# Six norms ahead of the linears: squares summed into columns of tokens, root and reciprocal taken on those, the result spread by a matmul

## The reference, cut to what matters

```python
def rms_norm(x, g=None):
    xf = x.astype(F32)
    y = xf * lax.rsqrt(jnp.mean(xf * xf, axis=-1, keepdims=True) + EPS)
    ...
def modulate(h, shift, scale):
    return h * (1.0 + scale) + shift
...
h @ w_in
```

## Time and profile before

| what | value |
|---|---|
| median of 3 runs | 3646.12 us (3642.33 to 3648.9) |
| the profiled execution | 3642.8 us, its span 3641.0 us |
| mean granted TensorE clock | 0.909 of full speed |
| TensorE matmul busy | 3077.7 us (85%), 15844 instructions |
| weight loads busy | 2512.0 us (69%) |
| VectorE busy | 1320.7 us (36%) |
| ScalarE busy | 1020.9 us (28%) |
| GpSimd busy | 961.4 us (26%) |

### The profile page before, as it was taken

One profiled execution on the slowest core, in us unless ns is written; L12 is line 12 of the kernel. 1 busy time (PEld: TensorE's weight loads), 2 busy tenths in 40 slices (PEclk: granted clock), 3 DMA queues, 4 the chain that ended last, 5 costly groups with the idle time before them and its releaser, 6 DMA issues. The chain is left out here.

```text
span 3641.0 us, 40685 instructions
## 1 busy us (share of the span) xinstructions
PE 3077.7 (85%) x15844; PEld 2512.0 (69%) x15844; DVE 1320.7 (36%) x1888; ACT 1020.9 (28%) x1443; POOL 961.4 (26%) x308
## 2 busy tenths in 40 slices
PE   2888976588998998899989999998967777988697
PEld 1667876476887887779547767876856665778475
DVE  7264636523155126040133164113544445101412
ACT  2244234213311211322023232223322223323432
POOL 0101211022222322643013334432423222330132
PEclk7889986688999999999999999999989888999798
DMA  4101410011133135422102243222200001220021
GB/s 176 40 1 58 157 58 1 1 49 56 54 137 127 58 108 198 145 81 84 43 22 82 81 179 136 101 82 74 89 22 0 0 0 47 93 88 24 22 84 58
DMA packets 48509, 265.33 MB, mean 73 GB/s; under 512 B 5380, under 2 KB 6660, under 8 KB 28420
## 3 DMA queue, kind: packets, MB, share of 16 engines
q1 hardware_dynamic: 48384, 263.63, 20.3%
HBM read 261.51 MB, written 2.10 MB: 72 GB/s over the span
## 5 line engine op out<-in xcount | busy, mean ns | idle before, releaser
L378 POOL TENSOR_TENSOR shared_w_lo<-stage,shared_w_hi 128x2048 fp32r<-128x2048 f32 (+2 forms) x179 | 783.6, 4378 | 1968.1 <-ACT shared_w_hi L351 1955.9
L351 ACT CAST shared_w_hi<-stage 128x2048 fp32r<-128x2048 f32 (+2 forms) x179 | 319.6, 1787 | 519.7 <-PEq L332 147.9
L418 PE MATMUL f0i_acc<-norm_b_hi,shared_w_hi 128*128 128x512 f32 x704 | 186.1, 346 | 27.8 <-PEq L332 14.5
L418 PE MATMUL f0i_acc<-norm_b_lo,shared_w_hi 128*128 128x512 f32 x704 | 184.8, 344 | 0.0
L418 PE MATMUL f1i_acc<-norm_e_hi,shared_w_hi 128*128 128x512 f32 x352 | 140.1, 398 | 9.5 <-DVE norm_e_lo L526 8.0
L418 PEld LDWEIGHTS f0i_acc<-norm_b_hi,shared_w_hi 128*128 128x128 f32 x704 | 110.2, 193 | 46.9 <-issue 25.0
L418 PE MATMUL f1i_acc<-norm_e_lo,shared_w_hi 128*128 128x512 f32 x352 | 138.9, 394 | 0.0
L618 DVE TENSOR_TENSOR ffn_hidden<-f0i_acc,ffn_gate 128x512 f32<-128x512 f32 (+1 forms) x44 | 22.5, 553 | 307.5 <-PE f0i_acc L418 307.5
L418 PE MATMUL f0i_acc<-norm_b_hi,shared_w_lo 128*128 128x512 f32 x704 | 130.3, 338 | 0.0
L608 ACT CAST ffn_hi<-ffn_hidden 128x768 f32 (+3 forms) x44 | 32.0, 728 | 330.2 <-DVE ffn_hidden L618 330.2
L418 PEld LDWEIGHTS f0i_acc<-norm_b_lo,shared_w_hi 128*128 128x128 f32 x704 | 110.6, 193 | 16.1
(11 more groups left out here) (536 smaller groups left out, 7262.4 us busy)
## 6 DMA issues: line engine op xcount, KB each, us to landing
stage<-in_w_f0i SPq DMA_DIRECT2D x22, 1024.0 KB, 4.8
stage<-in_w_f1i SPq DMA_DIRECT2D x22, 1024.0 KB, 4.8
mod_slots_d<-in_w_mod SPq DMA_DIRECT2D x32, 512.0 KB, 3.7
stage<-in_w_rv SPq DMA_DIRECT2D x16, 1024.0 KB, 4.8
mod_slots_b<-in_w_mod SPq DMA_DIRECT2D x24, 512.0 KB, 4.3
mod_slots_c<-in_w_mod SPq DMA_DIRECT2D x24, 512.0 KB, 3.4
stage<-in_w_rqk SPq DMA_DIRECT2D x12, 1024.0 KB, 4.8
mod_slots_e<-in_w_mod SPq DMA_DIRECT2D x24, 512.0 KB, 5.5
```

The lines of the kernel that those rows point to most:

```text
L351: nc.scalar.copy(w_hi[:, slot, 0:size], stage[:, slot, 0:size]).then_inc(hi_ready, 1)
L378: nc.gpsimd.tensor_tensor(w_lo[:, slot, 0:size], stage[:, slot, 0:size], w_hi[:, slot, 0:size].bitcast(F32), ALU.subtract)\
L418: mm = nc.tensor.matmul(out[0:min(P, nt), b, 0:m], w[:, k, unit[1]:unit[1] + min(P, nt)], x[:, k, s:s + m], start=begin, stop=end)
```

## The change

The operands of the summing matmul trade places: the squares, 128 tokens of them at a time, are the stationary operand and one column of ones is the moving one, so that the sums of 128 tokens come out as one column with a token in each partition. The columns of a norm (6, 2 or 4) are neighbouring elements in the second PSUM bank of the norm's tile. ScalarE takes the root of those few elements, VectorE the reciprocal in place, and TensorE spreads them: the column, repeated 128 times, is the stationary operand, and the identity is the moving one, so that every partition of `rstd`, now in PSUM, has each token's value. Two waits are new: TensorE waits for the reciprocal before it spreads (and the linear's matmuls stand behind that), and VectorE waits for the spread.

```diff
-                rstd = sb(scope, f"norm{n}_rstd", [P, T])
+                root = sb(scope, f"norm{n}_root", [P, T // P])
+                rstd = psum(scope, f"norm{n}_rstd", [P, 2, 512])
+                columns = rstd[:, 1, 504:504 + T // P]
                 scaled = squares
-                total = psum(scope, f"norm{n}_total", [P, 2, 512])
...
                     act.wait_ge(S["summed"], done["summed"] + DC)
-                    for b, (s, m, _, _) in enumerate(groups):
-                        last = nc.scalar.activation(rstd[:, s:s + m], total[:, b, 0:m], ACT.Sqrt, bias=eps_col,
-                                                    scale=1.0 / D)
-                    last.then_inc(S["root"], 1)
+                    nc.scalar.activation(root[:], columns, ACT.Sqrt, bias=eps_col, scale=1.0 / D).then_inc(S["root"], 1)
...
                     for c in range(DC):
                         pe.wait_ge(S["squares"], done["squares"] + c + 1)
-                        for b, (s, m, _, _) in enumerate(groups):
-                            mm = nc.tensor.matmul(total[:, b, 0:m], ones[:], squares[:, c % 2, s:s + m],
-                                                  start=c == 0, stop=c == DC - 1)
+                        for b in range(T // P):
+                            mm = nc.tensor.matmul(columns[:, b:b + 1], squares[:, c % 2, b * P:(b + 1) * P], ones[:, 0:1],
+                                                  start=c == 0 and b == 0, stop=c == DC - 1 and b == T // P - 1)
                         mm.then_inc(S["summed"], 1)
+                    pe.wait_ge(S["rstd"], done["rstd"] + 1)
+                    for b in range(T // P):
+                        mm = nc.tensor.matmul(rstd[:, b // 4, b % 4 * P:(b % 4 + 1) * P],
+                                              root[:, b:b + 1].broadcast_to([P, P]), ident[:], start=True, stop=True)
+                    mm.then_inc(S["spread"], 1)
...
                     dve.wait_ge(S["root"], done["root"] + 1)
-                    nc.vector.reciprocal(rstd[:], rstd[:]).then_inc(S["rstd"], 1)
-                    dve.wait_ge(S["rstd"], done["rstd"] + 1)
+                    nc.vector.reciprocal(root[:], root[:]).then_inc(S["rstd"], 1)
+                    dve.wait_ge(S["spread"], done["spread"] + 1)
...
-                        for s, m, a, _ in groups:
+                        for b, (s, m, a, _) in enumerate(groups):
                             last = nc.vector.scalar_tensor_tensor(
-                                scaled[:, c % 2, s:s + m], x_of(c, s, m), a(c), rstd[:, s:s + m],
+                                scaled[:, c % 2, s:s + m], x_of(c, s, m), a(c), rstd[:, b, 0:m],
                                 ALU.mult, ALU.mult)
```

More of the change, by code:

```diff
@@ L460, in feature_units @@
             return [("F", c, segs) for c in range(0, nt, P)]
-        norm_sem = {k: sem("norm_" + k) for k in ("squares", "summed", "root", "rstd", "scaled", "hi", "lo")}
+        norm_sem = {k: sem("norm_" + k) for k in ("squares", "summed", "root", "rstd", "spread", "scaled", "hi", "lo")}
         norms = [0]
@@ L548, in source @@
                 return dict(act=of_act, pe=of_pe, dve=of_dve, ready=S["lo"], first=done["lo"])
-            for k, m in (("squares", DC), ("summed", DC), ("root", 1), ("rstd", 1), ("scaled", DC), ("hi", DC),
+            for k, m in (("squares", DC), ("summed", DC), ("root", 1), ("rstd", 1), ("spread", 1), ("scaled", DC), ("hi", DC),
                          ("lo", DC)):
```

## The result

The changed kernel takes 3663.47 us, the median of 8 runs (3659.73 to 3672.46); the kernel before, measured with it, 3647.9 us (3642.33 to 3656.54). The ratio is 1.0044 with a 95% interval of 1.0031 to 1.0058: 16 us slower, where 17 were forecast. The profiled execution's span is 3663.6 us against 3641.0.

The account below looks back on a forecast made before the run. The six norms' chains of sums, root, reciprocal and first scaling were taken to bound the kernel; a +5.1, b +4.6, c -0.6, d +2.3, e +2.9, f +2.7 gave +17 us on 3646.1: 3663 us, range 3651 to 3677.

Parts of the forecast that it names:

- The pace: Sums of the norms: weight loads set 0.21 us an instruction at half clock, 20.35 us over 768 tokens, 13.6 over 512.
- The clock: TensorE in the sums of all six norms: granted clock stays at 0.50, 1.2 GHz.
- the rule named there: Trainium skill: recent busyness sets TensorE's clock, so loading and multiplying without a gap would be given 2.4 GHz.
- The 13.50 us at 0.50: Earlier trace, 678.00 to 691.50: TensorE busy throughout with matmuls of 64 and 128 columns, yet the clock stayed at 0.50.
- The tails: From each norm's last sum to its first scaling: 3.3, 2.45 and 1.6 us, 0.7 to 2.8 us shorter than before.
- All of it on the path: Sums, root, reciprocal and first scaling of each norm are a chain, every microsecond of it one of the kernel's.
- PSUM and the linear's start: Scalings that read `rstd` from PSUM cost nothing more, and nothing is lost again at the linear's start.
- Rival 1: Clock rises to 1.00 within the sums, 0.11 us an instruction: -16 us, 3630 us; chance 0.08.
- Rival 2: Rows and columns together set the sums' pace, 0.12 us an instruction at half clock: -18 us, 3628 us; chance 0.05.
- the 16 x 16 row: Earlier trace: four 16 x 16 matmuls with 16 rows of weights in 0.39 us, 0.06 us each at full clock.
- Rival 3: Accumulating into one column stalls each second instruction of a pair in the sums, 0.4 us: +40 us, 3703 us; chance 0.04.
- rival 4: Clock high in about half of the sums, TensorE coming warm from the linear before; gain and loss cancel: 3646 us; chance 0.04.

Follow-up runs that it names:

- Experiment 3: The changed kernel with four float32 matmuls of 512 columns more on TensorE ahead of the sums in norms b to f: 3654.63 us, ratio 1.0015.
- Experiments 1 and 2: The changed kernel with 128 (1) or 64 (2) columns of ones as moving operand of the sums: 3629.52 us, run again 3632.84 us (1); 3664.6 us (2).
- Experiment 5: The changed kernel with each matmul of the sums issued a second time into columns that nobody reads: 3751.48 us, ratio 1.0283.
- experiments 4 and 6: Four float32 matmuls ahead of the sums in norms b to f: changed kernel with 128 columns of ones (4), 3632.61 us; kernel before (6), 3647.37 us.
- experiment 9: The changed kernel with 128 columns of ones and two float32 matmuls of 512 columns ahead of the sums in norms b, e and f: 3619.41 us, ratio 0.9934.

## Why the prediction was right

The forecast was 3663 us, the measured median 3663.47. That they are this close is luck in part: the forecast set out from 3646.1 us, and the kernel before, measured beside the changed one, took 3647.9; the change was forecast at 17 us, and the medians say 15.6. The two misses cancel, and from one set of runs to the next the medians of the kernel before differed by 5 us. The steps stand on their own:

- **The pace.** 0.21 us an instruction from the earlier trace rows, 0.213 measured, for one column as for 64 and 128. 20.35 us were forecast over 768 tokens, 20.61 and 20.64 measured; 13.6 over 512, 13.82 and 13.81 measured in d and e.
- **The clock.** Taken as 0.50 in all six, against the rule named there. It was 0.50 but for the start of norm f, whose sums took 13.00 us; a has no clock record, and the pace of its matmuls is that of b. The prediction named two reasons, the few columns and the idle time before the norms, and both count. Experiment 3 takes the idle time away, and the clock still falls in four of five norms. Experiments 1 and 2 show that the loads alone do not bring the clock: with the same loads and no gap in either, the sums with 64 moving columns stayed at 1.2 GHz, and those with 128 rose to 2.4 GHz. The 13.50 us at 0.50 from which the prediction argued had two matmuls of 64 columns for each of 128; that 128 alone would rise could not be read from them.
- **The tails** were forecast 0.25 us too short each: 3.55, 2.68 and 1.83 us measured for 3.3, 2.45 and 1.6. The root of 6, 4 or 2 elements took 0.26 us and not 0.22, and the eight matmuls of the spread 2.08 and not 1.9, since the second of them starts 0.38 us after the first and not 0.21.
- **All of it on the path.** Experiment 5: 416 instructions more cost what 416 instructions last.
- **PSUM and the linear's start** cost nothing: a scaling of 512 takes 0.748 us from PSUM, 0.752 before, and 2.44 us lie between the first scaling and the linear's first matmul, as before.
- **Rival 1** was wrong for this kernel and right for experiment 1, with 3630 us forecast and 3629.52 and 3632.84 measured: it had the price of a high clock, which the one column kept from coming true.
- **Rival 2** falls by the pace of 0.213. A narrow moving operand alone did not make the 16 x 16 row fast, since here it has one column. The four matmuls of that row are transposes (L1910), one instruction each, and their weight loads are shorter too:

```profile
L1910 PEld LDWEIGHTS dn_p_cols<-ident,dn_beta_a_rows x4: 133/137/138, 2659.5 to 2659.7; 16*128 16x128 f32 x4
...
L913 PEld LDWEIGHTS win_p_turned<-ident,win_row x160: 138/140/145, 209.2 to 299.4; 128*128 128x128 f32 x160
...
L925 PEld LDWEIGHTS win_p_mixed<-v_pad,win_probs x320: 190/192/192, 212.1 to 301.6; 128*128 128x128 f32 x160
```

All three are at 2.4 GHz. The load of a transpose with 16 rows of weights lasts 137 ns, that of a transpose with 128 rows (L913) 140 ns, and that of a float32 matmul (L925) 192 ns: the row was of another kind of operation than the sums, and its price did not carry over. By the Trainium skill, "TensorE: Matmul & The Clock Gate", "LDWEIGHTS (loading the stationary operand)", the rows of the weights don't matter for the time of a load. The 137 and 140 ns agree with that. The transposes of L913 start 0.11 us apart and those of L1910 0.06; they differ in rows and in moving columns, and no run here separates the two.
- **Rival 3** falls by the even starts within a float32 matmul (experiment 5), **rival 4** by the clock: of the 320 summing matmuls of b to f, 9 ran at 2.4 GHz, where this rival had about half.
- What stays open is the 3 us by which the sum of the norms (+18.7) and the medians (+15.6, by the ratio 11 to 21) differ; it lies within the interval.

## What to carry to other kernels

Before a wide operation is turned round so that it streams few columns, price the weight loads, and ask what TensorE's clock will be: a float32 matmul whose moving operand has 1 or 64 columns kept to 1.2 GHz here where a run of them without a gap began at that clock (for 41 us in norm b of experiment 5) and fell to it where it began at 2.4 GHz (experiment 3), and the same one with 128 columns cost no more at 1.2 GHz and came to 2.4 GHz within the sums. The idea behind the change was sound (root and reciprocal of a few elements in place of tens of thousands saved 1 to 4 us a norm at the same clock), and padding the moving operand to the width that the weight load hides anyway turned 16 us lost into 15 to 21 won by the medians. Matmuls that only fill a dead stretch win what the higher clock gives back, less what they delay the real work: ending too late, they won 9 to 12 us in experiment 3 and nothing in experiments 4 and 6; in experiment 9, where they ended in time, they delayed nothing.

## What the runs showed of the hardware that was not expected

- Sums that began at 2.4 GHz, behind the four matmuls, kept it for a part of their length: in experiment 3, 47 of the 96 one-column matmuls of norm b, 49 of the 64 of norm e and all 32 of norm c ran at it. Without the matmuls ahead the clock was low from the first one in b to e and high for the first 9 in f.
- Two float32 matmuls of 512 columns, 1.96 us, held the clock over gaps of 0.5 us (norms e and f) and 0.8 us (norm b) before the sums in experiment 9.
